# Every fourth and every eighth V row of an expert layer scaled and added on VectorE instead of PE

## The reference

```python
hf = rmsnorm(x, g_ffn)                         # tokens in blocks of 128
q = (hb @ w_q).reshape(128, 8, 2, 64)
sc = einsum('thpd,hpnd->thpn', q, sub_keys)
# top 16 of each half, then top 16 of the 256 sums: experts e, scores top_s
gate = softmax(top_s)
act = gelu(einsum('thkd,td->thk', u_tab[e], hb))
y = einsum('thk,thkd->td', gate * act, v_tab[e])
x = x + y;  out = rmsnorm(x, g_final)
```

## Time and profile before

| | |
|---|---|
| median of three runs (lowest, highest) | 3562.11 us (3547.14 to 3569.12) |
| the profiled execution's own time | 3551.95 us |
| its span, first to last instruction | 3550.2 us |
| mean granted clock of PE | 0.962 of full speed |
| busy: PE, PEld, DVE | 3170.8, 1613.1, 2105.7 us |
| busy: ACT, POOL | 1612.3, 1270.6 us |
| moved by DMA | 1295.00 MB, 365 GB/s over the span |

### The profile page before, as it was taken

How to read it: one execution, slowest core, us unless ns; L and a number is a source line. 1 busy time by engine, 2 the same in 40 slices (tenths; PEclk the granted TensorE clock), 3 DMA queues, 4 the chain that set the end, 5 groups by cost and what they waited for, 6 DMA issues and landing times.

```text
span 3550.2 us, 33864 instructions
## 1 busy us (share of the span) xinstructions
PE 3170.8 (89%) x10190; PEld 1613.1 (45%) x10190; DVE 2105.7 (59%) x5347; ACT 1612.3 (45%) x4383; POOL 1270.6 (36%) x1097
## 2 busy tenths in 40 slices
PE   6989999998989998998999889988898888978887
PEld 5655555543445444554445334543354344533222
DVE  1256637675576457663767477656755376645954
ACT  2146324554455344652556345644564355423433
POOL 0023324343443334342434344334334343323442
PEclk8999999999999999999999999999999999989999
DMA  4269989999999999999999999999989998889998
GB/s 172 92 268 359 383 341 408 391 408 411 372 420 360 399 375 418 371 394 364 406 403 377 402 400 421 337 400 396 420 314 390 354 367 313 331 314 356 411 422 351
DMA packets 234350, 1295.00 MB, mean 365 GB/s; under 512 B 45700, under 2 KB 66084, under 8 KB 91446
## 3 DMA queue, kind: packets, MB, share of 16 engines
q0 software_dynamic: 156672, 1140.92, 80.4%
q1 hardware_dynamic: 77494, 151.92, 11.6%
HBM read 1275.74 MB, written 16.44 MB: 364 GB/s over the span
## 4 chain that ended last, share of the span: by engine, by line
PE 56%; DMA 24%; DVE 12%; ACT 4%; SPq 2%; issue 2%; POOL 0%; DVEq 0%; ACTq 0%
PE PS L972 30%; DMA R<-in_t_uv,idx 8%; PE PS L679 7%; DMA wring<-in_w_out 6%; DVE R L1600 5%; DMA wring<-in_w_query 4%; DMA R<-in_t_uv,idxS 3%; PE PS L918 3%; PE PS L945 3%; PE PS L645 3%; PE PS L760 2%; PE PS L759 2%; PE PS L741 2%; SPq L376 2%; DMA R<-in_cache_krope 1%
## 5 line engine op out<-in xcount | busy, mean ns | idle before, releaser
L972 PE MATMUL PS<-R,diag 128*128 128x512 f32 x4352 | 2055.1, 612 | 158.4 <-ACT diag L1230 116.2
L612 POOL DMA_INDIRECT R<-in_t_uv,idx x1024 | 1206.2, 1178 | 2158.0 <-PE PS L972 1834.2
L1600 DVE CUSTOM_DVE_ANT_0 R<-R,hb 128x1024 f32<-128x1024 f32 x1088 | 1316.5, 1221 | 765.8 <-DMA R<-in_t_uv,idx 682.4
L972 PEld LDWEIGHTS PS<-R,diag 128*128 128x128 f32 x4352 | 802.1, 194 | 1168.8 <-issue 756.2
L1223 ACT ACTIVATE acts<-dots 128x1 f32<-128x1 f32 x1088 | 215.2, 198 | 865.1 <-DVE dots L1600 862.6
L1230 ACT ACTIVATE diag<-ident,wv 128x128 f32<-128x128 f32 x1024 | 411.3, 402 | 248.0 <-PE PS L972 216.1
L1225 ACT ACTIVATE wv<-gate,acts 128x1 f32<-128x1 f32 x1024 | 301.4, 294 | 33.2
L679 PE MATMUL PS<-R 128*128 128x256 f32 (+1 forms) x1280 | 284.9, 378 | 16.6 <-DMA R<-in_t_win 11.3
L679 PEld LDWEIGHTS PS<-R 128*128 128x128 f32 x1280 | 240.1, 194 | 76.9 <-issue 35.7
L918 PE MATMUL PS<-wring,T 128*128 128x512 f32 x256 | 143.2, 688 | 90.9 <-DMA wring<-in_w_out 90.0
L1341 DVE CUSTOM_DVE_ANT_0 PP<-PS,mask 128x144 f32<-128x144 f32 (+7 forms) x64 | 49.5, 773 | 247.4 <-PE PS L760 247.2
(11 more groups left out here) (235 smaller groups left out, 2352.1 us busy)
## 6 DMA issues: line engine op xcount, KB each, us to landing
...
R<-in_t_uv,idx POOLq DMA_INDIRECT x1024
...
```

What stands on the lines that cost most here:

```text
L612: e.indirect_dma_start(dst, None, table, bass.IndirectOffsetOnAxis(ap=index, axis=0)).then_inc(S[s], c.count(name, s, 16))
L972: m = mm(bank(n), diag[:, s % DR, :], pair(s)[:, D + 512 * n:D + 512 * n + 512], start=begins, stop=s == last_slot(t), skip_group_check=True)
L1600: e.tensor_tensor_reduce(u, u, hb[:, tile_of(g) % 2, :], 1.0, 0.0, ALU.mult, ALU.add, dots[:, g % NW:g % NW + 1]).then_inc(dve_done, c.cou ...
```

## The change

A slot s of the prompt tiles is on DVE when s % 4 == 2 for s % 128 in 4 to 59, or s % 8 == 2 elsewhere. For such a slot ACT makes the weight in wv and no diagonal, PE does nothing, and DVE in turn s + 2, behind that turn's U product, computes x = V * wv + x straight into the residual xb with one scalar_tensor_tensor over 1024 columns. It waits for ACT's weight and for the one before it of its tile (the first of a tile waits for the norm that last read xb). POOL's wait for the last reader of a buffer goes to DVE for these slots. PE's slots number the diagonals by their own count. The sum at a tile's end gets a wait for DVE's own last instruction.

```diff
--- before.py
+++ after.py
@@ -71,6 +71,15 @@
 
 def last_slot(t):
     return P * t - 1 if t <= NTILE else NSLOT - 1
+
+
+def on_dve(s):
+    return s < P * NTILE and s % (4 if 4 <= s % P < 60 else 8) == 2
+
+
+BY_PE = [s for s in range(NSLOT) if not on_dve(s)]
+BY_DVE = [s for s in range(NSLOT) if on_dve(s)]
+NTH = {s: i for q in (BY_PE, BY_DVE) for i, s in enumerate(q)}
 
 
 def stage(st, t):
@@ -257,6 +266,9 @@
         def pair(s):
             return R[:, 2 * (s % RN):2 * (s % RN) + 2, :].rearrange("p a d -> p (a d)")
 
+        def spent(c, s):
+            return (dve_done, c.at("dve", f"x{s}")) if on_dve(s) else (pe_done, c.at("pe", f"v{s}"))
+
         def gate_of(s):
             t = tile_of(s)
             return gateS[:, s - P * NTILE:s - P * NTILE + 1] if t == SMP else gate[:, t % 2, s % P:s % P + 1]
@@ -625,7 +637,7 @@
                 if s < RN:
                     e.wait_ge(pe_done, c.at("pe", f"P0_{max(i for i, x in enumerate(ITEMS[0]) if x[0] == s)}"))
                 else:
-                    e.wait_ge(pe_done, c.at("pe", f"v{s - RN}"))
+                    e.wait_ge(*spent(c, s - RN))
                 if s == P * NTILE:
                     e.wait_ge(dve_done, c.at("dve", "idxS"))
                 elif t < SMP and s % P % (P // pieces(t)) == 0:
@@ -959,7 +971,7 @@
 
             def peer(g):
                 s = g - LAG
-                if not 0 <= s < NSLOT:
+                if not 0 <= s < NSLOT or on_dve(s):
                     return
                 t = tile_of(s)
                 begins = s == P * (t - 1)
@@ -969,7 +981,7 @@
                     e.wait_ge(act_done, c.at("act", f"P0_{len(ITEMS[0]) - 1}"))
                 e.wait_ge(act_done, c.at("act", f"d{s}"))
                 for n in range(2):
-                    m = mm(bank(n), diag[:, s % DR, :], pair(s)[:, D + 512 * n:D + 512 * n + 512],
+                    m = mm(bank(n), diag[:, NTH[s] % DR, :], pair(s)[:, D + 512 * n:D + 512 * n + 512],
                            start=begins, stop=s == last_slot(t), skip_group_check=True)
                 m.then_inc(pe_done, c.count(f"v{s}"))
 
@@ -1222,12 +1234,14 @@
                     e.wait_ge(dve_done, c.at("dve", f"u{v}"))
                     act(acts[:, k:k + 1], dots[:, k:k + 1], ACT.Gelu).then_inc(act_done, c.count())
                     settle()
-                    act(wv[:, k:k + 1], gate_of(v), ACT.Copy, scale=acts[:, k:k + 1]).then_inc(act_done, c.count())
-                    settle()
-                    if v >= DR:
-                        e.wait_ge(pe_done, c.at("pe", f"v{v - DR}"))
-                    m = fold if tile_of(v) == SMP else ident
-                    act(diag[:, v % DR, :], m[:], ACT.Copy, scale=wv[:, k:k + 1]).then_inc(act_done, c.count(f"d{v}"))
+                    act(wv[:, k:k + 1], gate_of(v), ACT.Copy, scale=acts[:, k:k + 1]).then_inc(act_done, c.count(f"w{v}"))
+                    if not on_dve(v):
+                        settle()
+                        n = NTH[v]
+                        if n >= DR:
+                            e.wait_ge(pe_done, c.at("pe", f"v{BY_PE[n - DR]}"))
+                        m = fold if tile_of(v) == SMP else ident
+                        act(diag[:, n % DR, :], m[:], ACT.Copy, scale=wv[:, k:k + 1]).then_inc(act_done, c.count(f"d{v}"))
                 for t in range(1, SMP + 1):
                     if g == last_slot(t) + LAG + 1:
                         e.wait_ge(dve_done, c.at("dve", f"ysum{t}"))
@@ -1599,6 +1614,17 @@
                     u = pair(g)[:, 0:D]
                     e.tensor_tensor_reduce(u, u, hb[:, tile_of(g) % 2, :], 1.0, 0.0, ALU.mult, ALU.add,
                                            dots[:, g % NW:g % NW + 1]).then_inc(dve_done, c.count(f"u{g}"))
+                v = g - LAG
+                if 0 <= v < NSLOT and on_dve(v):
+                    t, n = tile_of(v), NTH[v]
+                    e.wait_ge(act_done, c.at("act", f"w{v}"))
+                    if n and tile_of(BY_DVE[n - 1]) == t:
+                        e.wait_ge(dve_done, c.at("dve", f"x{BY_DVE[n - 1]}"))
+                    else:
+                        e.wait_ge(dve_done, c.at("dve", f"h{t}"))
+                    x = xb[:, t % 2, :]
+                    stt(x, pair(v)[:, D:2 * D], wv[:, v % NW:v % NW + 1], x, ALU.mult, ALU.add).then_inc(
+                        dve_done, c.count(f"x{v}"))
 
             run(dict(prep=prep, kv=kv, meta=meta, q=q, att=att, ret=ret, atts=atts, rets=rets, out=out, norm2=norm2, top=top),
                 peer)
```

## The result

The changed kernel took 3512.48 us, median of 4 runs (3506.78 to 3516.36). The kernel before took 3557.81 in 4 runs beside them (3547.14 to 3569.12). The ratio is 0.9871 with a 95% interval of 0.9843 to 0.9899, so 45 us or 1.3% faster. The forecast was a fall of 97 us from the median. The sign was right and the time lies in the range, but less than half of the forecast gain came.

What follows compares the result with a forecast made beforehand. DMA at 421 GB/s was taken to bound turns 90 to 117, PE the attention turns. Gains of 79 + 21 - 6 = 94 us took the profiled 3552 to 3458; with the median 10 us higher, it said 3465, range 3400 to 3562.

Steps and rivals of the forecast that it cites:

- attention, tiles 1 to 7: Turns 5 to 59: PE loses 24.8 us per stretch, stretches end 5% above DMA's floor; 66.8 us gained.
- attention, tile 8: Turns 5 to 59 of tile 8, with the sample sequences' chain: half of 24.8 us taken, 12.4 gained.
- turns 60 to 89, all tiles: Where w_out and w_query are streamed: 42 us of PE relief, half counted for weight and norm waits, 21 gained.
- VectorE and everything else: 6 us charged for VectorE's new instructions, in tile 8's turns 90 to 117, tiles' first five turns and badly timed moments.
- The bound and the floors: DMA's ceiling is 421 GB/s; PE is late in attention, whose eight stretches have floors totalling 1154 of 1307 us.
- the allowance of 5% above the floor: Attention stretches of tiles 1 to 7 were set 5% above DMA's floor, as tile 2 stood 6% above.
- The marks that I named: Attention, tiles 2 to 7: 148 to 157 us, 395 GB/s or more, PE under 0.93; V passes 3616; VectorE near 1.28 us.
- Rivals 1 and 3: First: DMA already binds in attention, 3557, chance 0.14. Second: VectorE binds in attention, 3607, chance 0.10.
- rival 3: In attention and sample sequences, VectorE's new instruction waits for ScalarE's weight, delaying each head 3.5 us: 3607, chance 0.10.
- Rival 2: In attention the head's chain binds before DMA, PE idles at a lower clock; 3521, chance 0.16.

Runs made afterwards that it cites:

- experiment 7: Changed kernel with VectorE's 184 V rows left out of the sum, buffers freed at ScalarE's weight: 3474.93 us, ratio 0.9772.
- Experiment 10: Changed kernel with every fourth row on VectorE in turns 4 to 89 only, none from turn 90 of tile 7, page table loaded early: 3495.25 us, ratio 0.9818.
- experiment 6: Kernel before the change with only the page table's load moved earlier in SP's queue: 3557.56 us, ratio 0.9988.
- Experiment 4: Changed kernel with the page table's load moved earlier in SP's queue: 3498.91 us, ratio 0.9833.
- experiment 2: Changed kernel with the 28 VectorE rows from turn 90 of tile 7 on given back to PE: 3495.5 us, ratio 0.9817.
- experiment 5: Changed kernel with no VectorE rows from turn 90 of tile 7 on and the page table loaded early: 3479.91 us, ratio 0.9787.
- 1 again: The changed kernel measured and profiled once more, no edit: 3513.76 us, ratio 0.9872.
- 3 attention only: Changed kernel with VectorE rows only in each tile's attention turns, the other 72 back on PE: 3506.44 us, ratio 0.9852.

## Why the prediction was right and wrong

The forecast's terms beside what the two profiles measured (us gained):

| term | forecast | measured |
|---|---|---|
| attention, tiles 1 to 7 | 66.8 | 77.4 |
| attention, tile 8 | 12.4 | -19.3 |
| turns 60 to 89, all tiles | 21 | 7.4 |
| VectorE and everything else | -6 | -29.9 |
| sum | 94 | 35.6 |

Cut at turn 90 of tile 7 the account is plainer. The early part was to gain 85 us less a share of the 6, and gained 76.7. The late part was to gain 15 less the rest, and lost 42.1. So nearly the whole miss lies in the late part.

**The bound and the floors were right.** I took 421 GB/s as the ceiling and said that attention turns would come down towards time x GB/s / 421. Tiles 2 to 6 reached 146.0 to 149.2 us at 408 to 419 GB/s. The seven attention stretches of tiles 1 to 7 were forecast at 66.8 us and measured at 77; the allowance of 5% above the floor was somewhat too much in tiles 2 to 6, and tile 1 gained only 2.9 of 12.8. The marks that I named came too (passes at 3616, 1281 ns, rates over 395), except that PE's share stayed up to 0.96 in place of under 0.93.

**Rivals 1 and 3 fell.** DMA was not the bound before: its share rose from 0.95 to 0.99 to 1.00 and 1.01, and with it the rate from 375 to 396 up to 408 to 419. The new instruction waited for 30.7 us in 7 places where rival 3 needed 64 long waits, and experiment 7 shows attention as long without it. Rival 2's number (3521) is near the result, but its mechanism isn't what happened: in tiles 2 to 6 PE is busy for 0.88 to 0.96 and the stretches lie within 2% of DMA's floor. Its remark that an idler PE shows a lower clock did come out, in the late part (0.94 to 0.86) and over the whole span (0.962 to 0.933).

**Turns 60 to 89: the size was off.** I took half of 42 us, 21. Tiles 1 to 7 gained 11 (783.8 to 772.8), and with tile 8 it is 7.4 us, as the sum of the eight stretches shows beside the one in rows 5:

```profile
sum 903.40, PE 746.80 PEld 343.84 DVE 382.87 ACT 279.99 POOL 267.18; mean PE 93.35 PEld 42.98 DVE 47.86 ACT 35.00 POOL 33.40
```

Experiment 10 speaks for the reason that the prediction gave for taking half: these turns are bound mostly by something else than PE. Which thing that is, no run shows.

**The step that failed: tile 8.** "In tile 8, where the sample sequences' chain keeps PE at 0.85 only, I take half of the 24.8, 12.4." Tile 8's attention took 19 us more, and the late part took 42 us more (583.7 and 583.2 in two profiles, against 541.6, and 547.4 in experiment 6). The 42 are the surer number: experiment 6, with no row on VectorE and the time of the kernel before, took 177.6 us for tile 8's attention alone, where the kernel before took 164.6. I had read that chain as a reason for a smaller gain. It should have been read as the thing that binds there: a chain of small loads, products and masks, whose links go through SP's queue and VectorE. PE's relief gives such a chain nothing, and both of the change's side effects hit it.

- About 20 us: the sequences begin later against their surroundings. The page table lands after a wait of 11.1 us in place of 3.6, so the cache loads come 8.5 us later, and eight of twenty then fall into the time after turn 90 in which an issue takes 1.5 to 5.9 us. Experiment 4 takes this back (63.5 to 43.2), 6 shows that it is no gain of its own, and 7 that it comes from the relief and not from VectorE's load.
- About 17 us after the sequences go back when VectorE's 28 rows in the late part go back to PE (337.0 to 320.9 in experiment 2 and 322.5 in 5). The 3.7 us within the sequences are less than one profile can tell (172 to 190 us over all kernels).

The 17 us, cut at turns 60, 90 and 118 of tile 8 (differences of starts as in the table of the experiments, us):

| kernel | last mask to 59 | 60-89 | 90-117 | 118 on |
|---|---|---|---|---|
| before | 97.7 | 127.1 | 75.7 | 19.6 |
| after | 105.5 | 130.7 | 80.5 | 20.3 |
| 1 again | 105.5 | 133.1 | 80.5 | 20.0 |
| 2 none late | 98.7 | 126.5 | 75.7 | 19.9 |
| 3 attention only | 105.0 | 126.9 | 75.7 | 20.9 |
| 5 both 2 and 4 | 97.1 | 128.7 | 75.7 | 21.1 |
| 7 rows left out | 97.9 | 134.3 | 75.7 | 20.4 |

In the first piece all five kernels with rows on VectorE there take 102.9 to 105.5 us and the seven without 96.5 to 99.3. In turns 90 to 117 the four with such rows take 80.5 and the eight without 75.7. Together these are 12 to 13 of the 17 us, and they are gone in experiment 7 as in experiment 2, so they are VectorE's. Turns 60 to 89 spread over 124 to 134 us with no pattern, and hold most of the rest. The first piece before, after and with the rows left out:

```profile
3058.00:3155.70 97.70, 80.40 (x407) 46.01 (x407) 76.04 (x133) 36.99 (x109) 36.72 (x29) 0.90 0.86 323
3005.50:3111.00 105.50, 75.25 (x379) 44.82 (x379) 85.56 (x142) 35.93 (x106) 40.22 (x29) 0.83 0.85 309
2972.80:3070.70 97.90, 72.92 (x379) 43.83 (x379) 76.08 (x133) 35.70 (x106) 38.83 (x29) 0.84 0.86 327
```

VectorE is busy for 9.5 us more there and the piece is 7.8 us longer, though VectorE's share is only 0.81. I read that as VectorE standing in the sequences' chain there. The lower clock isn't the cause, since the third row keeps the old length at 0.84. In turns 90 to 117 I had set 4.0 us of free time against 5.1 of work; VectorE is now full there, busy 78.78 of 80.50 us, and four new instructions cost nearly all of their 5.1.

The stretch in question, with turns 90 to 117 of tile 5 and 0 to 4 of tile 6, answers to rows 3:

```profile
2020.70:2094.40 73.70, 53.72 (x120) 20.96 (x119) 66.60 (x196) 31.89 (x100) 34.80 (x29) 0.98 1.01 422
2117.30:2132.40 15.10, 9.54 (x16) 3.54 (x14) 14.02 (x48) 7.99 (x19) 2.96 (x4) 0.77 1.01 420
3241.70:3322.20 80.50, 54.29 (x96) 19.28 (x95) 78.78 (x218) 28.50 (x84) 31.40 (x29) 0.83 0.95 385
```

**VectorE's cost was mis-sized.** I charged 6 us; experiment 7 puts it at 36 to 39 at most, 25 of them in the late part. In the early part the first five turns of tiles 3 to 7 went from 13.6 us before to 15.0, and take 13.8 in experiment 7, where a free time of 1.0 us should have left 0.3 of the 1.28. In an almost full stretch one more instruction costs nearly its whole length.

With both losses taken away (experiment 5) the program is 81 us faster where I had forecast 97. The mechanism was right where I worked it out stretch by stretch, and wrong where I put a share of it on a stretch that something else binds.
